# A hybrid-decoder layer on one core: x1 stored earlier, a weight sum made by an adding DMA, products reordered, the last transposes spread out

## The chip, the cores and the metric

The kernel runs on one core of one Trainium2 chip. The metric is the device time of one execution in microseconds, median of the runs. The profile is of one execution.

## The reference, cut to what matters

With DEPTH = 1 only layer 0 runs: sparse attention over a compressed latent, a LayerNorm, a SwiGLU feed-forward, a second LayerNorm. Sequence 256, width 2048, feed-forward width 5632, all float32.

```python
m = _dsa_mixer(x, *mix_p)
x = _layer_norm(DEEPNORM_ALPHA * x + m, ln1_g, ln1_b)          # called x1 below
x = _layer_norm(DEEPNORM_ALPHA * x + (silu(x @ w_gate) * (x @ w_up)) @ w_down, ln2_g, ln2_b)
```

The change touches the feed-forward alone.

## The kernel before, in words

**Splitting.** Every float32 operand is split into a high part (ScalarE, an ACTIVATE Copy to fp32r) and a low part (VectorE, raw minus high), and each product is three matmuls (high x high, high x low, low x high) of 128 x 128 by 128 x 512. A *step* is one weight block of 1024 columns per partition: ScalarE makes its high part, VectorE its low part, TensorE multiplies. The split blocks live in w_hi and w_lo, rings of RING = 4 places. So the high part of step v is made only when TensorE has finished step v - 4, and each engine runs through the steps in one written order, `FFN_STEPS`.

**Gate and up.** The 5632 hidden columns are 22 tiles of 256 (gate and up columns side by side, 512 columns). Tiles 0 and 1 are plain. The other 20 are 10 pairs, p = 1 to 10. In each pair the first four of the 16 inner blocks go by a Strassen-Winograd scheme: seven products in place of eight, over four weight blocks B11, B12, B21, B22 of two 512-column parts, which arrive in one place (`quad`), and sums of them, T1 to T4, made in that place (`pair_sum`, L1378). The remaining 12 blocks are plain steps: six called "first" and six called "second", for the two tiles of the pair. A product step is 6 matmuls, a plain step is 12.

**The sums of weights.** T1 = B11 + B12 replaces B11 and is read by product P5. T3 = B12 + B22 replaces B12 (P7). T2 = T1 + B22 replaces T1 (P6). T4 = T2 + B21 replaces B21 (P4). P1 reads B11, P2 reads B21, P3 reads B22. VectorE makes all four sums and counts them in pair_t_done, and ScalarE's `hi_step` (L955) waits for the count.

**The sums of results.** PSUM is short, so results are passed on by copies. `before_hi` (L972) is what ScalarE does ahead of the high part of step v. The loop there makes three copies per pair ("seeds", semaphore `seeded`), each at the step four places after its product: after P1 it copies the bank second[:, 1] to first[:, 0], after P6 the same bank, negated, to second[:, 0], after P7 the same bank to first[:, 1]. P6 and P7 add into second[:, 1] themselves, so P6 must not begin before the first seed is made, and P7 not before the second. P2 adds into first[:, 0], P3 into second[:, 0], P4 into first[:, 1]. In `pair_product` (L1945) TensorE waits on `seeded` ahead of P6, P7 and P4, and in `pair_plain` (L1968) ahead of "first" 0.

```python
for n, dst, sign in ((P1, first[:, 0, :], 1.0), (P6, second[:, 0, :], -1.0),
                     (P7, first[:, 1, :], 1.0)):
    if v == V_OF[p, "product", n] + RING:
```

The order of a pair p of 2 to 10 is P1, second 3, P5, second 4, P6, second 5, P7, P2, P3, first 0, P4, first 1 to 5, second 0 to 2; the three "second" steps in front belong to pair p - 1. Pair 1 has nothing between: P1, P5, P6, P7, P2, P3, first 0, P4.

**x1 and the factor sums.** The sums of x1 that the products need are made by GpSimd (g_sum) and split by ScalarE (L950) and GpSimd (L1577) into s_gate. s_gate lies on the bytes of xn, which holds x1. So x1 is first stored to DRAM (L669, 2 MB, semaphore x1_stored) and is read back at the end (L682). ScalarE's copy into s_gate stands after the high part of half 6 of tile 1 and waits for the store. SyncE's DMA queue, in order, is: tile 0, the two quad loads of pair 1, tile 1, four plain loads of pair 1 (each waiting for a low part of tile 1), the store of x1, then the rest.

**Down.** The hidden activations of a pair are transposed by VectorE (`turn_hid`, L1341, 16 STREAM_TRANSPOSE in four batches of four), split by ScalarE (`hid_hi`) and VectorE (`hid_lo`), and their sums are made by GpSimd (loop at L1581, with ScalarE's L1003). The down projection runs as 158 units, plain (12 matmuls, 1024 weight columns) or product (3 matmuls, 512 columns); the first four are plain. Of a quad's seven products VectorE makes a weight sum after each of the first four (`t_sum`, L1424). The last pair is transposed in units 3 to 6, a batch in each, its high part is made after unit 8 and its low part before unit 9.

Of the kernel before, what the change touches and what calls it, by code (L numbers as in the profile page):

```python
# [27 lines left out]
ALU = mybir.AluOpType  # L28
# [5 lines left out]
TOK = S // P  # L34
# [117 lines left out]
def ffn_sequence():  # L152

    steps = []
    for p in range(1, PAIRS):
        ends = [(p - 1, "second", n) for n in range(PLAIN - 3, PLAIN)] if p > 1 else [None] * 3
        for product, end in zip((P1, P5, P6), ends):
            steps += [(p, "product", product), end]
        steps += [(p, "product", n) for n in (P7, P2, P3)] + [(p, "first", 0), (p, "product", P4)]
        steps += [(p, "first", n) for n in range(1, PLAIN)] + [(p, "second", n) for n in range(PLAIN - 3)]  # L160
    steps += [(PAIRS - 1, "second", n) for n in range(PLAIN - 3, PLAIN)]
    return tuple(step for step in steps if step)
# [54 lines left out]
DOWN_SLOTS, DOWN_UNITS = down_plan()  # L217
RING_BLOCKS = 2 * RING
LAST_LATE = RING


def ring_places():
# [45 lines left out]
def layer_kernel(nc, a):  # L268
    ctx = ExitStack()
    with ctx:  # L270
# [198 lines left out]
        g_hi = sem("g_hi")  # L469
        g_lo = sem("g_lo")  # L470
        pair_t_done = sem("pair_t_done")
        seeded = sem("seeded")
        y_taken = sem("y_taken")
        y_added = sem("y_added")
# [116 lines left out]
        def _(sp):  # L591
# [71 lines left out]
            for q in range(2):  # L663
                load_quad(1, q)
            load_tile(1)
            for n in range(PLAIN_SLOTS):
                load_plain(1, n)
            sp.wait_ge(x1_done, TOK * CHUNKS)
            sp.dma_start(x1_rows, xn[:]).then_inc(x1_stored, 16)  # L669
            for p in range(1, PAIRS):  # L670
                for n in range(PLAIN_SLOTS if p == 1 else 0, 2 * PLAIN):
                    load_plain(p, n)
# [30 lines left out]
        def _(act):  # L703
# [251 lines left out]
            def hi_step(p, kind, n):  # L955

                v = V_OF[p, kind, n]
                if kind == "product":
                    if n == P1:
                        for q in range(2):  # L960
                            act.wait_ge(quad_full[q], 16 * p)
                    elif n in SUM_OF:
                        act.wait_ge(pair_t_done, 4 * (p - 1) + SUM_OF[n] + 1)
                    act.wait_ge(*used_step(v - RING))
                    act.activation(by_quad(w_hi[:, v % RING, :]), quad(p, SOURCE[n]), ACT.Copy).then_inc(hi_done, 1)  # L965
                else:
                    m = plain_index(p, kind, n)
                    act.wait_ge(plain_full[m % PLAIN_SLOTS], 16 * (m // PLAIN_SLOTS + 1))
                    act.wait_ge(*used_step(v - RING))
                    act.activation(w_hi[:, v % RING, :], plain_raw(m), ACT.Copy).then_inc(hi_done, 1)  # L970
# [50 lines left out]
            for u in range(len(DOWN_UNITS)):  # L1021
                down_hi_unit(u)
                if u == 2:
                    silu_step(TILES - 1)
                if u == 8:
                    hid_hi(PAIRS - 1)
                for pair in range(DOWN_PAIRS):
                    if u == FIRST_REST[2 * pair] + 2:
                        if pair > 0:
                            act.wait_ge(fold_done, FOLDS * pair)  # L1030
                        act.wait_ge(*used_unit(LAST_PRODUCT[pair]))
                        act.activation(hid[:, 0, :, :].rearrange("p t f -> p (t f)"), tp[:, 0, :],
                                       ACT.Copy).then_inc(u2_seeded, 1)
# [11 lines left out]
        def _(dve):  # L1045
# [292 lines left out]
                dve.tensor_tensor(hid[:, i % 2, :, :], hid[:, i % 2, :, :], banks_of(i)[:, :, FC:2 * FC],  # L1338
                                  ALU.mult).then_inc(ffn_hid, 1)

            def turn_hid(p, b):  # L1341

                if b == 0:
                    dve.wait_ge(ffn_hid, 2 * p + 2)
                    dve.wait_ge(y_added, 2 * min(p + 1, PAIRS - 1))
                    if p > 0:
                        dve.wait_ge(s_step, 4 * min(p, len(DOWN_QUADS)))
                for n in range(4):
                    src = hid[32 * n:32 * n + 32, :, :, :].rearrange("p i t (c f) -> p i t c f", c=2)
                    dst = turned[32 * b:32 * b + 32, :, :, :].rearrange("p i c (t s) -> p i t c s", t=TOK)  # L1350
                    last = dve.transpose(dst[:, :, :, :, 32 * n:32 * n + 32], src[:, :, :, :, 32 * b:32 * b + 32])  # L1351
                if b == 3:
                    last.then_inc(ffn_turned, 1)

            def hid_lo(p):
# [45 lines left out]
            for p, kind, n in FFN_STEPS:  # L1401
                before_lo(V_OF[p, kind, n])
                lo_step(p, kind, n)
                if (kind, n) == ("product", P1):
                    pair_sum(p, B11, B11, B12)
                    pair_sum(p, B12, B12, B22)
                if (kind, n) == ("product", P5):
                    pair_sum(p, B11, B11, B22)
                if (kind, n) == ("product", P2):
                    pair_sum(p, B21, B11, B21)  # L1410
                if (kind, n) == ("first", 2):
                    add_y(p)
                if kind == "first" and n >= 2:
                    turn_hid(p - 1, n - 2)
# [49 lines left out]
            for u in range(len(DOWN_UNITS)):  # L1464
                if u == 3:
                    gate_up(TILES - 1)
                if u == 9:
                    hid_lo(PAIRS - 1)
                down_lo_unit(u)
                if DOWN_UNITS[u][4][0] == "product":  # L1470
                    t_sum(u)
                if 3 <= u < 7:
                    turn_hid(PAIRS - 1, u - 3)
                for pair in range(DOWN_PAIRS):
                    rest = u - FIRST_REST[2 * pair]
                    if 3 <= rest < 7:
                        fold(pair, 2 * rest - 6)
                        fold(pair, 2 * rest - 5)
                if u in (FIRST_REST[1] + 3, FIRST_REST[1] + 4):
                    down_residual(0, u - FIRST_REST[1] - 3)  # L1480
                if u in (PAIR_FIRST[1] + 3, PAIR_FIRST[1] + 4):
                    down_residual(1, u - PAIR_FIRST[1] - 3)
# [40 lines left out]
        def _(pool):  # L1523
# [53 lines left out]
            pool.tensor_tensor(s_gate[:, 1, :, :, :], g_sum[:], s_gate[:, 0, :, :, :], ALU.subtract).then_inc(g_lo, 1)  # L1577

            a11, a12, a21, a22 = (turned[:, 0, c, t * P:(t + 1) * P] for t in range(TOK) for c in range(2))
            for q in range(len(DOWN_QUADS)):  # L1580
                if q > 0:  # L1581
                    pool.wait_ge(s_lo, q)
                pool.wait_ge(ffn_turned, q + 1)
                pool.tensor_tensor(s_sum[:, S3, :], a11, a21, ALU.subtract).then_inc(s_step, 1)
                pool.wait_ge(s_step, 4 * q + 1)
                pool.tensor_tensor(a21, a21, a22, ALU.subtract).then_inc(s_step, 1)
                pool.wait_ge(s_step, 4 * q + 2)
                pool.tensor_tensor(s_sum[:, S2, :], a21, a11, ALU.subtract).then_inc(s_step, 1)
                pool.wait_ge(s_step, 4 * q + 3)
                pool.tensor_tensor(s_sum[:, S4, :], a12, s_sum[:, S2, :], ALU.add).then_inc(s_step, 1)  # L1590
                pool.wait_ge(s_hi, q + 1)
                pool.tensor_tensor(s_t[:, q, 1, :, :], s_sum[:], s_t[:, q, 0, :, :], ALU.subtract).then_inc(s_lo, 1)

            pool.wait_ge(xt_full, TOK * CHUNKS)
            pool.affine_select(out=ident[:], in_=ident[:], compare_op=ALU.not_equal, fill=-1.0, base=0,
# [4 lines left out]
        def _(pe):  # L1600
# [344 lines left out]
            def pair_product(p, n):  # L1945

                first, second = banks_of(2 * p), banks_of(2 * p + 1)
                out = {P1: second[:, 1, :], P5: tp[:, 2, :], P6: second[:, 1, :], P7: second[:, 1, :],
                       P2: first[:, 0, :], P3: second[:, 0, :], P4: first[:, 1, :]}[n]
                v = V_OF[p, "product", n]  # L1950
                start = n in (P1, P5)
                if n == P1:
                    pe.wait_ge(ffn_hid, max(1, 2 * p - 2))
                if n == P5:
                    pe.wait_ge(g_lo, 1)
                    if p > 1:
                        pe.wait_ge(y_taken, p - 1)
                if n in (P6, P7, P4):
                    pe.wait_ge(seeded, 3 * p - 2 + (P6, P7, P4).index(n))
                pe.wait_ge(lo_done, v + 1)  # L1960
                for q in range(2):
                    for x, part in ((0, w_hi), (0, w_lo), (1, w_hi)):
                        last = pe.matmul(out, factor(q, Q_FACTOR[n], x), part[:, v % RING, q * GC:(q + 1) * GC],  # L1963
                                         start=(start and (q, x) == (0, 0) and part is w_hi),
                                         stop=((q, x) == (1, 1)), skip_group_check=not start)
                last.then_inc(pe_used, 1)
# [161 lines left out]
```

## Time and profile before

| | us |
|---|---|
| median of 3 runs (lowest, highest) | 940.78 (938.51, 940.89) |
| the profiled execution | 940.2 |
| its span | 938.4 |
| mean granted TensorE clock | 0.998 of full speed |

The span is from the first to the last instruction, and 1.8 us lie around it. Attention and the output projection take the first 224 us, tile 0 and tile 1 run to about 270, the ten pairs to 698 and the down projection to 930. An engine's busy time in a table is not its load: matmuls overlap, and TensorE is busy nearly always in this kernel. What tells of lost time is a gap ahead of a weight load (PEld), and the place where the chain of waits leaves TensorE.

### The profile page before, as it was taken

How to read it: one execution, taken by the hardware profiler on the slowest of the kernel's cores; microseconds unless marked ns; L12 is line 12 of the kernel's file. 1: busy time of each engine (PE TensorE's matmuls, PEld its weight loads, DVE VectorE, ACT ScalarE, POOL GpSimd, SP SyncE). 2: the span in 40 equal slices, each digit the busy share in tenths (PEclk: the TensorE clock that was granted, in tenths of full speed). 3: DMA queues.
4: the chain of work that ended last, by engine and by line, in shares of the span. 5: the costliest groups of instructions: out<-in, count | busy, mean ns of one | idle time of the engine just before them, and what ended most of it. 6: DMA issues, size and time to landing. Idle time of an engine off the chain costs nothing.

```text
span 938.4 us, 11643 instructions
## 1 busy us (share of the span) xinstructions
PE 926.8 (99%) x4406; PEld 775.0 (83%) x4406; DVE 775.2 (83%) x1049; ACT 513.5 (55%) x704; POOL 95.6 (10%) x84
## 2 busy tenths in 40 slices
PE   9999999999989999999999999999999999999997
PEld 8999988888868888888888888888887888888885
DVE  6778566578668898989999999988969987799777
ACT  5686765353445646465565646465545564465550
POOL 0205530000311010202021011000000000000000
PEclk9999999999999999999999999999999999999999
DMA  9844324584617474756647474656665666355632
GB/s 361 317 157 150 121 90 179 180 352 170 213 71 252 129 271 124 258 171 214 231 147 255 125 269 133 248 177 220 224 211 238 257 235 233 133 207 231 236 133 90
DMA packets 36759, 188.06 MB, mean 200 GB/s; under 512 B 4064, under 2 KB 4576, under 8 KB 22880
## 3 DMA queue, kind: packets, MB, share of 16 engines
q1 hardware_dynamic: 36672, 187.32, 55.9%
q8 instruction: 35, 0.57, 0.3%
q14 instruction: 20, 0.16, 0.0%
q0 software_dynamic: 32, 0.00, 0.0%
HBM read 183.11 MB, written 4.19 MB: 200 GB/s over the span
## 4 chain that ended last, share of the span: by engine, by line
PE 94%; DVE 4%; DMA 1%; ACT 1%; issue 0%; DVEq 0%; SPq 0%; ACTq 0%
PE acc L1980 26%; PE acc L2002 19%; PE acc L1755 9%; PE tp L1980 9%; PE acc L1963 6%; PE acc L1693 5%; PE tp L1963 4%; PE acc L1614 4%; PE tp L2002 4%; PE acc L1892 2%; PE acc L1727 1%; DVE w_lo L1204 1%; PE tp L1806 1%; DMA out<-xn 1%; PE tp L1741 1%; DVE turned L1351 1%
## 5 line engine op out<-in xcount | busy, mean ns | idle before, releaser
L1980 PE MATMUL acc<-w_hi,act_t 128*128 128x512 f32 x720 | 227.3, 389 | 0.0
L970 ACT ACTIVATE w_hi<-raw 128x1024 fp32r<-128x1024 f32 x120 | 125.9, 1058 | 108.8 <-PE acc L1980 51.9
L1019 ACT ACTIVATE w_hi<-raw 128x512 fp32r<-128x512 f32 (+1 forms) x154 | 114.7, 782 | 98.4 <-PE acc L2002 83.8
L2002 PE MATMUL acc<-w_hi,hid_t 128*128 128x512 f32 x504 | 161.3, 390 | 0.1
L1422 DVE TENSOR_TENSOR w_lo<-raw,w_hi 128x512 fp32r<-128x512 f32 (+1 forms) x154 | 131.7, 882 | 35.8 <-ACT w_hi L1019 35.4
L1980 PEld LDWEIGHTS acc<-w_hi,act_t 128*128 128x128 f32 x720 | 135.1, 188 | 28.0
L1375 DVE TENSOR_TENSOR w_lo<-raw,w_hi 128x1024 fp32r<-128x1024 f32 x120 | 148.1, 1252 | 6.9 <-ACT w_hi L970 6.1
L1980 PE MATMUL acc<-w_lo,act_t 128*128 128x512 f32 x360 | 140.0, 389 | 0.0
L2002 PEld LDWEIGHTS acc<-w_hi,hid_t 128*128 128x128 f32 x504 | 94.6, 188 | 20.3 <-DVE w_lo L1422 0.8
L2002 PE MATMUL acc<-w_lo,hid_t 128*128 128x512 f32 x252 | 98.1, 389 | 0.0
L1372 DVE TENSOR_TENSOR w_lo<-raw,w_hi 128x1024 fp32r<-128x1024 f32 x63 | 82.8, 1314 | 17.8 <-ACT w_hi L965 17.5
L965 ACT ACTIVATE w_hi<-raw 128x1024 fp32r<-128x1024 f32 x63 | 66.7, 1058 | 46.1 <-DVE raw L1379 31.0
L1351 DVE STREAM_TRANSPOSE turned<-hid 32x256 f32<-32x256 f32 x176 | 76.7, 436 | 3.8
L1980 PEld LDWEIGHTS acc<-w_lo,act_t 128*128 128x128 f32 x360 | 67.6, 188 | 14.1
L1980 PE MATMUL tp<-w_hi,act_t 128*128 128x512 f32 x240 | 76.6, 389 | 0.0
L1755 PE MATMUL acc<-w_hi,o_t 128*128 128x512 f32 x224 | 73.4, 398 | 0.0
L1204 DVE TENSOR_TENSOR w_lo<-raw,w_hi 128x1024 fp32r<-128x1024 f32 x31 | 42.4, 1382 | 22.7 <-ACT w_hi L872 22.7
L2002 PEld LDWEIGHTS acc<-w_lo,hid_t 128*128 128x128 f32 x252 | 47.3, 188 | 9.8
L1980 PEld LDWEIGHTS tp<-w_hi,act_t 128*128 128x128 f32 x240 | 45.0, 188 | 9.3
L1755 PEld LDWEIGHTS acc<-w_hi,o_t 128*128 128x128 f32 x224 | 42.1, 188 | 8.6
L1980 PE MATMUL tp<-w_lo,act_t 128*128 128x512 f32 x120 | 46.7, 389 | 0.0
L1755 PE MATMUL acc<-w_lo,o_t 128*128 128x512 f32 x112 | 43.6, 390 | 0.0
(262 smaller groups left out, 1585.3 us busy)
## 6 DMA issues: line engine op xcount, KB each, us to landing
raw<-in_w_pairs SPq DMA_DIRECT2D x120, 512.0 KB, 4.4
raw<-in_w_down SPq DMA_DIRECT2D x44, 1024.0 KB, 5.7
raw<-in_w_pairs SPq DMA_DIRECT2D x18, 1024.0 KB, 7.6
raw<-in_w_out SPq DMA_DIRECT2D x16, 1024.0 KB, 4.9
raw<-in_w_gu SPq DMA_DIRECT2D x8, 1024.0 KB, 10.3
raw<-in_x_w SPq DMA_DIRECT2D x14, 552.0 KB, 7.1
raw<-in_w_uq SPq DMA_DIRECT2D x4, 1024.0 KB, 6.0
raw<-in_w_ukv SPq DMA_DIRECT2D x4, 1024.0 KB, 4.8
```

Source lines behind the costliest of these rows:

```text
L965: act.activation(by_quad(w_hi[:, v % RING, :]), quad(p, SOURCE[n]), ACT.Copy).then_inc(hi_done, 1)
L970: act.activation(w_hi[:, v % RING, :], plain_raw(m), ACT.Copy).then_inc(hi_done, 1)
L1019: act.activation(unit_parts(u)[0], block_of(b, block, width), ACT.Copy).then_inc(down_hi_done, 1)
L1204: dve.tensor_tensor(w_lo[:, h, 0:n], raw[:, slot, first:first + n], w_hi[:, h, 0:n], ALU.subtract).then_inc(lo_done, 1)
L1351: last = dve.transpose(dst[:, :, :, :, 32 * n:32 * n + 32], src[:, :, :, :, 32 * b:32 * b + 32])
L1372: dve.tensor_tensor(by_quad(w_lo[:, v % RING, :]), quad(p, LOW_OF[n]), by_quad(w_hi[:, v % RING, :]), ALU.subtract).then_inc(lo_done, 1)
L1375: dve.tensor_tensor(w_lo[:, v % RING, :], plain_raw(plain_index(p, kind, n)), w_hi[:, v % RING, :], ALU.subtract).then_inc(lo_done, 1)
L1422: dve.tensor_tensor(lo_, block_of(b, block, width), hi_, ALU.subtract).then_inc(down_lo_done, 1)
L1755: last = pe.matmul(acc[:, bank0 + t, :], lhs[:, k, x, t * P:(t + 1) * P], part[:, w, n * GC:(n + 1) * GC], start=(start and x == 0 and par ...
L1963: last = pe.matmul(out, factor(q, Q_FACTOR[n], x), part[:, v % RING, q * GC:(q + 1) * GC], start=(start and (q, x) == (0, 0) and part is w ...
L1980: last = pe.matmul(out[:, t, :], act_t[:, k0 + m, x, t * P:(t + 1) * P], part[:, v % RING, m * GC:(m + 1) * GC], start=False, stop=(end an ...
L2002: last = pe.matmul(bank, lhs(x), part[:, cols * GC:(cols + 1) * GC], start=(first == u and (cols, x) == (0, 0) and part is hi_), stop=(end ...
```

## The change

- SyncE issues the store of x1 ahead of the four plain loads of pair 1 instead of behind them.
- The order of a pair becomes P1, second 3, P2, second 4, P5, second 5, P6, P7, P3, first 0, P4, and so on; in pair 1 P1, P2, P5, P6, P7, P3, first 0, P4. TensorE waits for the first seed ahead of P2 instead of P6. The three copies of `before_hi` stay as they are, four places after P1, P6 and P7.
- T1 is no longer made by VectorE. GpSimd, once the low part of P1's block is made, issues a DMA that reads B12 from DRAM again (512 KB) and adds it to B11 in place. ScalarE waits for its landing (t1_full) ahead of P5's high part. VectorE makes T4 after P6 instead of after P2.
- GpSimd's loop over the factor sums is cut in two functions, and an adding DMA stands ahead of them in each pair.
- The 16 transposes of the last pair come one in each of units 4 to 19. Its high part is made after unit 22, its low part before unit 23.

```diff
-        for product, end in zip((P1, P5, P6), ends):
+        for product, end in zip((P1, P2, P5), ends):
             steps += [(p, "product", product), end]
-        steps += [(p, "product", n) for n in (P7, P2, P3)] + [(p, "first", 0), (p, "product", P4)]
+        steps += [(p, "product", n) for n in (P6, P7, P3)] + [(p, "first", 0), (p, "product", P4)]
...
+LAST_TURN = 20
...
             load_tile(1)
+            sp.wait_ge(x1_done, TOK * CHUNKS)
+            sp.dma_start(x1_rows, xn[:]).then_inc(x1_stored, 16)
             for n in range(PLAIN_SLOTS):
                 load_plain(1, n)
-            sp.wait_ge(x1_done, TOK * CHUNKS)
-            sp.dma_start(x1_rows, xn[:]).then_inc(x1_stored, 16)
...
+                    elif n == P5:
+                        act.wait_ge(t1_full, 16 * p)
                     elif n in SUM_OF:
-                        act.wait_ge(pair_t_done, 4 * (p - 1) + SUM_OF[n] + 1)
+                        act.wait_ge(pair_t_done, 3 * (p - 1) + SUM_OF[n])
...
-                if u == 8:
+                if u == LAST_TURN + 2:
                     hid_hi(PAIRS - 1)
...
                 if (kind, n) == ("product", P1):
-                    pair_sum(p, B11, B11, B12)
                     pair_sum(p, B12, B12, B22)
                 if (kind, n) == ("product", P5):
                     pair_sum(p, B11, B11, B22)
-                if (kind, n) == ("product", P2):
+                if (kind, n) == ("product", P6):
                     pair_sum(p, B21, B11, B21)
...
-                if u == 9:
+                if u == LAST_TURN + 3:
                     hid_lo(PAIRS - 1)
...
-                if 3 <= u < 7:
-                    turn_hid(PAIRS - 1, u - 3)
+                if LAST_TURN - 16 <= u < LAST_TURN:
+                    b, n = divmod(u - LAST_TURN + 16, 4)
+                    turn_hid(PAIRS - 1, b, (n,))
...
+            def load_t1(p):
+
+                pool.wait_ge(lo_done, V_OF[p, "product", P1] + 1)
+                b12 = by_quad(w_pairs[p - 1][:, 0:2 * RAW_ELEMS])[:, :, B12 * GC:(B12 + 1) * GC]
+                pool.dma_start(quad(p, B11), b12, accum_op=ALU.add).then_inc(t1_full, 16)
...
+            for p in range(1, PAIRS):
+                load_t1(p)
+                if 0 <= p - 2 < len(DOWN_QUADS):
+                    factor_low(p - 2)
+                if p - 1 < len(DOWN_QUADS):
+                    factor_sums(p - 1)
...
-                if n in (P6, P7, P4):
-                    pe.wait_ge(seeded, 3 * p - 2 + (P6, P7, P4).index(n))
+                if n in (P2, P7, P4):
+                    pe.wait_ge(seeded, 3 * p - 2 + (P2, P7, P4).index(n))
```

## Rows read from the trace of the kernel before

**Rows 1.** Busy time and share of the span of each engine, whole execution.
```profile
PE 926.8 (99%) x4406; PEld 775.0 (83%) x4406; DVE 775.2 (83%) x1049; ACT 513.5 (55%) x704; POOL 95.6 (10%) x84
```
**Rows 2.** Waits of weight loads, 262 to 300 us: total, times, longest.
```profile
PEld acc L1963 <- ACT acc L982: 4.2, 2, 2.9
PEld tp L1932 <- DVE w_lo L1204: 1.3, 1, 1.3
```
**Rows 3.** The same view, 696 to 735 us.
```profile
PEld tp L2002 <- DVE w_lo L1422: 1.8, 1, 1.8
PEld acc L2002 <- DVE w_lo L1422: 1.2, 3, 0.5
```
**Rows 4.** Chain of waits, 240 to 292 us: start, duration, what.
```profile
253.00 10.28 DMA out<-xn
...
276.74 2.94 PE acc L1963 x6
...
279.71 0.59 ACT acc L982
...
280.34 4.37 PE acc L1963 x18
...
287.43 1.36 PE acc L1963 x6
```
**Rows 5.** Timeline around tile 1: x1 finished, plain loads, first matmuls of tile 1, s_gate.
```profile
236.80 1.41 DVE L1271 SCALAR_TENSOR_TENSOR xn<-xn,small,ln_rows 128x512 f32<-128x512 f32 x2
...
247.59 5.37 SPq L649 DMA_DIRECT2D raw<-in_w_pairs  x4
...
247.94 0.39 PE L1932 MATMUL tp<-w_hi,act_t 128*128 128x512 f32 x1
...
263.30 1.06 ACT L950 ACTIVATE s_gate<-g_sum 128x1024 fp32r<-128x1024 f32 x1 [5.88 <-DMA out<-xn]
```
**Rows 6.** Chain of waits in pair 3: P1, second 3, second 5.
```profile
394.87 1.36 PE tp L1963 x6
396.23 2.72 PE acc L1980 x12
...
404.39 2.72 PE acc L1980 x12
```
**Rows 7.** Timeline of pair 3: two seeds, silu, a high part; the low part of P1.
```profile
396.33 0.58 ACT L982 ACTIVATE acc<-tp 128x512 f32<-128x512 f32 x1 [0.30 <-PE tp L1963]
...
404.43 0.58 ACT L982 ACTIVATE tp<-tp 128x512 f32<-128x512 f32 x1 [0.30 <-PE tp L1963]
...
407.15 0.60 ACT L933 ACTIVATE hid<-acc 128x512 f32<-128x512 f32 x1 [1.17 <-PE acc L1980]
407.64 1.05 ACT L970 ACTIVATE w_hi<-raw 128x1024 fp32r<-128x1024 f32 x1
...
390.65 1.22 DVE L1372 TENSOR_TENSOR w_lo<-raw,w_hi 128x1024 fp32r<-128x1024 f32 x1
```
**Rows 8.** DMA issues: KB each, median us from issue to landing.
```profile
raw<-in_w_pairs SPq DMA_DIRECT2D x120, 512.0 KB, 4.4
...
rms_g<-in_rms_g_t POOLq DMA_DIRECT2D x1, 3.0 KB, 3.7
```
**Rows 9.** Windows: length, busy of PE, PEld, DVE, ACT, POOL, clock, DMA share, GB/s.
```profile
264.00:282.00 18.00, 13.73 (x51) 9.82 (x51) 15.43 (x13) 9.76 (x12) 2.40 (x1) 0.91 0.00 0
390.00:402.00 12.00, 12.00 (x55) 9.94 (x54) 12.00 (x11) 6.97 (x8) 1.56 (x1) 1.00 0.43 138
```
**Rows 10.** Timeline of VectorE in the first down units.
```profile
702.69 0.69 DVE L1422 TENSOR_TENSOR w_lo<-raw,w_hi 128x512 fp32r<-128x512 f32 x1
703.30 0.69 DVE L1432 TENSOR_TENSOR raw<-raw 128x512 f32<-128x512 f32 x1
704.02 1.78 DVE L1351 STREAM_TRANSPOSE turned<-hid 32x256 f32<-32x256 f32 x4
705.81 0.69 DVE L1422 TENSOR_TENSOR w_lo<-raw,w_hi 128x512 fp32r<-128x512 f32 x1
708.94 1.23 DVE L1422 TENSOR_TENSOR w_lo<-raw,w_hi 128x1024 fp32r<-128x1024 f32 x1
```

More of the change, by code:

```diff
@@ L471, in layer_kernel @@
         pair_t_done = sem("pair_t_done")
+        t1_full = sem("t1_full")
         seeded = sem("seeded")
@@ L1339, in gate_up, with turn_hid @@
                                   ALU.mult).then_inc(ffn_hid, 1)
-            def turn_hid(p, b):
-                if b == 0:
+            def turn_hid(p, b, blocks=range(4)):
+                if b == 0 and 0 in blocks:
                     dve.wait_ge(ffn_hid, 2 * p + 2)
@@ L1347, in turn_hid @@
                         dve.wait_ge(s_step, 4 * min(p, len(DOWN_QUADS)))
-                for n in range(4):
+                for n in blocks:
                     src = hid[32 * n:32 * n + 32, :, :, :].rearrange("p i t (c f) -> p i t c f", c=2)
@@ L1351, in turn_hid @@
                     last = dve.transpose(dst[:, :, :, :, 32 * n:32 * n + 32], src[:, :, :, :, 32 * b:32 * b + 32])
-                if b == 3:
+                if b == 3 and 3 in blocks:
                     last.then_inc(ffn_turned, 1)
@@ L1579, in _, with factor_sums @@
             a11, a12, a21, a22 = (turned[:, 0, c, t * P:(t + 1) * P] for t in range(TOK) for c in range(2))
-            for q in range(len(DOWN_QUADS)):
+            def load_t1(p):
+                pool.wait_ge(lo_done, V_OF[p, "product", P1] + 1)
+                b12 = by_quad(w_pairs[p - 1][:, 0:2 * RAW_ELEMS])[:, :, B12 * GC:(B12 + 1) * GC]
+                pool.dma_start(quad(p, B11), b12, accum_op=ALU.add).then_inc(t1_full, 16)
+            def factor_sums(q):
                 if q > 0:
@@ L1590, in _, with factor_low @@
                 pool.tensor_tensor(s_sum[:, S4, :], a12, s_sum[:, S2, :], ALU.add).then_inc(s_step, 1)
+            def factor_low(q):
                 pool.wait_ge(s_hi, q + 1)
                 pool.tensor_tensor(s_t[:, q, 1, :, :], s_sum[:], s_t[:, q, 0, :, :], ALU.subtract).then_inc(s_lo, 1)
+            for p in range(1, PAIRS):
[4 more added lines that the diff above has]
+                    factor_sums(p - 1)
             pool.wait_ge(xt_full, TOK * CHUNKS)
```

## The prediction

> **What bounds the kernel now.** I read the shares by engine first. TensorE is busy 99% of the span and no other engine over 83% [rows 1], so time is won or lost only where TensorE stops. The view that shows this is the one of waits, read on the weight loads in successive windows: a weight load that stands idle is a real gap. From tile 1 to the end of the down projection there are two places. In pair 1 the weight loads wait 4.2 us on the seed copies of L982 and 1.3 us on a low part of tile 1 [rows 2]. At the start of the down projection they wait 1.8 and 1.2 us on VectorE's low parts [rows 3]. Between 290 and 697 us, nine pairs long, that view has no row: in pair 3 product steps of 1.36 us and plain steps of 2.72 us stand end to end [rows 6], a matmul each 0.227 us. So the change can win in two short places and has nothing to win in nine pairs, where anything that makes TensorE wait costs nine times.
>
> The chain of waits tells the cause in pair 1. The store of x1 takes 10.28 us to land [rows 4]; ScalarE waits 5.88 us for it in front of the s_gate copy [rows 5], and everything behind it is late. Then P6 takes 2.94 us instead of 1.36 at half clock (1.2 GHz, after gaps), and TensorE stands while the second seed is copied [rows 4]. Without any stop P1 would begin 8 x 2.72 us after tile 1's first matmul, at 247.94 + 21.76 = 269.70 [rows 5], and the pair's seven products and first 0 would end 7 x 1.36 + 2.72 = 12.24 us later, at 281.94. They end at 287.43 + 1.36 = 288.79 [rows 4]. Pair 1 loses 6.85 us.
>
> **Store of x1 ahead of the plain loads.** x1 is finished at 236.80 + 1.41 = 238.21, and the first plain load, which the store now precedes on SyncE, is issued at 247.59 [rows 5]. So SyncE's new wait holds up nothing. With the same 10.28 us the store lands near 248.5, and the s_gate copy finds it landed at 263.30 - 5.88 = 257.42 [rows 5]. ScalarE is then early for half 7 of tile 1, the wait of 1.3 us there goes, and P1 runs at 269.70. Were P5 and P6 then as punctual as in later pairs, nearly all of 6.85 us would be won but for the exposed second seed. What is late next is the new DMA.
>
> **The adding DMA, its duration D.** It is issued by GpSimd when P1's low part is made. No accumulating DMA is in this trace. From below: a plain 512 KB load lands in 4.4 us [rows 8]. From above: GpSimd's only DMA takes 3.7 us for 3 KB [rows 8]; this one reads 512 KB from DRAM, reads 512 KB of B11 and writes as much, so at most three times the moving part of a plain load; taking that part as 2.3 us (an estimate, about half of the 4.4) gives 3.7 + 6.9 = 10.6 us. I take 7, between them. In 264 to 282 us the DMA engines are idle, and at 390 to 402 us, where the DMA falls in pair 3, 43% busy [rows 9], so later ones may take a little longer.
>
> **Pair 1 with that DMA.** P1's high part needs half 4 of tile 1, done at 247.94 + 5 x 2.72 = 261.54. High part (1.05) and low part (1.22), durations as in [rows 7], end near 263.9; the DMA lands at L = 263.9 + D. Here stands the wait that is easily missed: the first seed comes four places after P1, in pair 1 that is behind the high parts of P5 and P6, and P2, now second, waits for this seed. The chain is L, high part of P5 1.05, low part 1.2, T2 sum 1.15, high part of P6 1.0, seed 0.6, with handovers of 0.03: P2 starts at L + 5.1. With D = 7 that is 276.0, against 271.06 at which P1 ends: 4.9 us of stop. P2, P5, P6 run to L + 9.2, the second seed is again directly ahead of P7 (0.8 us), and P7, P3, first 0, P4 take 6.8: the end is L + 16.8 = 287.7. A stop of this length was followed by half clock in the trace of before, P6 taking 1.58 us more [rows 4]; I add 1.5. That is 289.2 against 288.79: **+0.4 us**. All that the earlier store wins is spent on the adding DMA. With D = 4.4 it is -2.2, with 10.6 +4.0, and 1.5 less if the clock stays up.
>
> The Trainium skill, "DMA: Bandwidth & Descriptors", section "Anatomy of one DMA — SWDGE (gpsimd) path", puts such a DMA at about 2.0 us plus bytes over 436e3 per us, which is 3.2 us for 512 KB as an estimate; P5 would then not wait for it at all, and pair 1 would come out near -3 us. The DMA that GpSimd issues in this trace speaks against so little, with 3.7 us for 3 KB [rows 8].
>
> **The new order in pairs 2 to 10.** This is the largest term. First seed: made when P1 is done, 396.33 to 396.91 [rows 7], while P2 starts only after second 3, at 396.23 + 2.72 = 398.95. That costs nothing, margin 2 us. Second seed: before, second 5 (2.72 us, [rows 6]) lay between P6 and P7, and the copy of 0.58 us that starts 0.04 us after P6's end (404.43 against 404.39, [rows 6, 7]) was hidden by it. Now P7 follows P6 directly and must wait for this copy. In pair 1 of before the two stand like that, and the chain shows the price: P6 ends at 279.68, the copy runs 279.71 to 280.30, P7 begins at 280.34 [rows 4], 0.66 us. To this comes the lost overlap: a matmul lasts 0.39 us [rows 5] and the next usually begins after 0.23, so 0.16. And ScalarE comes late: at the step of first 0 it has silu and a high part to do after second 5 ends, 407.15 to 408.6 [rows 7], 1.49 us after that end, while P6 now ends 1.36 us after it; with the copy's own 0.04 that is 0.09 more. Together 0.91 us, nine times: **+8.2 us**. From below 9 x 0.66 = 5.9, from above 9 x 1.05 = 9.5. I see no gain in it that could offset this. Third seed: P7 ends 2.3 us after P6's successor could have begun, first 0 needs it two products later, margin some 0.7 us; nothing.
>
> **The adding DMA in pairs 2 to 10.** P1's low part ends at 391.87 [rows 7]. P5 now runs as third product, at 396.23 + 2.72 + 1.36 + 2.72 = 403.03 [rows 6], and needs high and low part, 2.3 us, before: landing by 400.7, so D up to 8.8 us is hidden; the longer chain over T2 to P6 allows 401.4. At 7 it costs nothing; above 8.8 each excess counts nine times. GpSimd's queue behind it: the low factor part and the next factor sums, wanted some 20 us later; nothing. ScalarE behind P5's wait: second 5's high part, a product later; nothing below the same bound. VectorE loses ten sums of 1.15 us, but no step of TensorE waits for it here, so that wins nothing.
>
> **The last transposes.** Before, 16 transposes in four batches of 1.79 us (704.02 to 705.81) fall in units 3 to 6 [rows 10], and units 6 to 12 come late: about 2.9 us [rows 3]. After, they cover units 4 to 19. A transpose costs 0.45 us, and where it follows another instruction 0.11 more: 703.30 to 704.02 is 0.72 where a sum normally takes 0.61 [rows 10]. Single, 16 x 0.56 = 9.0 us instead of 7.6. VectorE's work from 700.9 to the low part of unit 24: 5 plain low parts x 1.14, 16 product low parts x 0.6, 10 sums x 0.6, transposes 9.0, the low part of the hidden values 1.14, in all 31.4, to 732.3, without any wait. TensorE would want unit 24 at 708.87 + 4 x 2.72 + 16 x 0.68 = 730.6. So the debt isn't avoided but moved to units 18 to 24, about 1.7 us and, with VectorE's waits for ScalarE, up to 3. I take **0**, from -2.9 (all gone) to +1.
>
> **The sum.** 940.2 (profiled execution, span 938.4 and 1.8 around it; the median of the runs is 0.6 above it) + 0.4 + 8.2 + 0 = **948.8 us**.
>
> **Rivals.** *The adding DMA is late.* If it takes over 8.8 us beside the plain loads, P5 waits in every pair. At 10.6: pair 1 +4.0, nine times 1.8 = +16.2, seeds +8.2: 968.6. For it: nothing in the trace bounds it well, and GpSimd's DMA is slow for its size. Against: DMA engines are half idle where it falls. Chance 0.22. *The second seed costs little, and the change is faster.* If P7 did not stand for the copy (a seed below 0.1 us of stop per pair), only pair 1 and the down start would count: with D = 5, pair 1 -1.6 and -1.5 for the clock, down -1: 936.1 to 939. It turns faster where the nine stops sum to less than about 4 us. Against it speaks P7 of pair 1, which stands in just this way [rows 4]. Chance 0.08. *The change does less than it says*: the page's short DMA and the down debt all gone give 940.2 + 8.2 - 3.3 - 2.9 = 942.2, the same within what can be told. Chance 0.07. The forecast itself (seed exposed, DMA in time): 0.63.
>
> **How the numbers follow.** About 0.3% (2.8 us) is what a measurement of this kernel can tell from no change. Slower by more: 0.63 + 0.22 = 0.85; within it 0.08; faster 0.07. The forecast's own range runs from 5.9 - 2.2 - 1.5 + 0 to 9.5 + 2.4 (D = 9) + 1, that is 942.4 to 953. Reaching for the late DMA, the range is 943 to 965.
>
> **What would show it.** Ahead of P7 (L1963) nine gaps of near 1 us, released by ScalarE's L982; ahead of P2 in pair 1 a gap of 3 to 8 us with the same releaser, and behind it ScalarE's L965 waiting for GpSimd's DMA; no wait for the store; the DMA's landing time under 9 us; VectorE as the releaser near units 18 to 24. The prediction is wrong if pairs 2 to 10 show no row of waits, or if ScalarE waits for the DMA with weight loads idle behind it in each pair.

## The result and the profile after

| | us |
|---|---|
| before, median of 4 runs | 939.64 (938.3 to 940.89) |
| after, median of 4 runs | 950.61 (950.02 to 950.78) |
| ratio, 95% interval | 1.0116 (1.0100 to 1.0132) |
| span of the profiled execution, before and after | 938.4 and 948.9 |

The change costs 11 us. The times of the kernel before fall in groups by the mean granted clock: in 23 executions of it on one chip those at 1.000 took 937.3 to 938.7 us and those at 0.996 took 940.5 to 941.2, while all four of the changed kernel were at 0.998. Busy shares hardly move; VectorE has ten sums less, GpSimd ten DMAs more:

```profile
PE 928.8 (98%) x4406; PEld 774.4 (82%) x4406; DVE 765.2 (81%) x1039; ACT 515.8 (54%) x704; POOL 108.1 (11%) x94
```

The view that answers to [rows 2, 3] is again the one of the weight loads' waits (who waited for whom, total, times, longest). From 262 to 300, 300 to 708 and 708 to 750 us it says of the changed kernel:

```profile
PEld acc L1985 <- ACT acc L986: 6.1, 2, 5.0
...
PEld tp L1985 <- ACT tp L986: 5.9, 5, 1.2
PEld acc L1985 <- ACT acc L986: 4.7, 4, 1.2
...
PEld acc L2024 <- DVE w_lo L1425: 2.4, 2, 1.2
PEld tp L2024 <- DVE w_lo L1425: 1.1, 1, 1.1
```

L986 is the seed copy (L982 before). The middle pair of rows is new: nine waits of 1.2 us in the stretch that had none. The chain of waits of pair 3 (start, duration, what) answers to [rows 6], and shows one of them. The piece at 405.45 is P5, the one at 406.81 second 5, and the one at 411.66 P7 with P3 behind it:

```profile
405.45 1.36 PE tp L1985 x6
406.81 2.73 PE acc L2002 x12
409.55 0.02 issue
409.57 0.02 ACT hid L935
409.59 0.47 issue
410.06 0.91 ACT w_hi L974
410.97 0.04 issue
411.01 0.60 ACT tp L986
411.61 0.04 issue
411.66 3.02 PE tp L1985 x12
```

The chain leaves TensorE at the end of second 5, goes through silu, the high part of first 0 and the seed on ScalarE and comes back at P7. P6 itself runs beside it and isn't in the chain. In the timeline P6's last matmul starts at 410.50 and P7's first at 411.66: 1.16 us where 0.23 is usual.

Pair 1, the same view:

```profile
263.99 6.22 DMA quad<-in_w_pairs
270.21 0.02 issue
270.23 1.07 ACT w_hi L969
271.30 0.02 issue
271.32 1.23 DVE w_lo L1376
272.55 1.15 DVE quad L1383
...
274.68 0.59 ACT acc L986
275.27 0.04 issue
275.31 2.82 PE acc L1985 x6
278.13 1.78 PE tp L1985 x6
...
287.68 1.36 PE acc L1985 x6
```

The store of x1 has left the chain of [rows 4], and the adding DMA stands in its place: it lands 6.22 us after its issue, then come P5's high part, its low part, the T2 sum, P6's high part, and at last the first seed, for which P2 waits 5.0 us. P2 takes 2.82 us instead of 1.36 after that stop, and P5 1.78: the granted clock was 0.58 from 275 to 278 us and 0.78 from 278 to 280. P4 ends at 289.04, against 288.79 before.

The sums agree: pair 1 +0.25; nine pairs at a distance of (671.05 - 325.16) / 8 = 43.24 us between the P7s of pairs 2 and 10, against 42.16, +9.7; start of the down projection 3.5 us of waits instead of 3.0, +0.5. That is 10.45 of the 10.5 us of span.

The DMA issues (KB each, median us to landing) answer to [rows 8]:

```profile
raw<-in_w_pairs SPq DMA_DIRECT2D x120, 512.0 KB, 4.7
raw<-in_w_pairs POOLq DMA_DIRECT2D x9, 512.0 KB, 6.1
out<-xn SPq DMA_DIRECT2D x1, 2048.0 KB, 10.0
```

### The profile page after: what moved, and what is told of

It is laid out like the page before. It is cut to its first block, busy times and chain, and to the rows that moved or that the text cites. A ratio compares the mean times of both kernels' runs of the same rounds, so it can differ in the third digit from the quotient of the medians.

```text
span 948.9 us, 11643 instructions
## 1 busy us (share of the span) xinstructions
PE 928.8 (98%) x4406; PEld 774.4 (82%) x4406; DVE 765.2 (81%) x1039; ACT 515.8 (54%) x704; POOL 108.1 (11%) x94
## 4 chain that ended last, share of the span: by engine, by line
PE 93%; DVE 3%; ACT 2%; issue 1%; DMA 1%; DVEq 0%; ACTq 0%
PE acc L2002 26%; PE acc L2024 18%; PE acc L1777 9%; PE tp L2002 9%; PE acc L1985 5%; PE acc L1715 5%; PE acc L1636 4%; PE tp L1985 4%; PE tp L2024 3%; PE acc L1914 2%; DVE w_lo L1425 2%; PE tp L1954 1%; PE acc L1749 1%; PE tp L1828 1%; ACT w_hi L974 1%
## 5 line engine op out<-in xcount | busy, mean ns | idle before, releaser
L1379 DVE TENSOR_TENSOR w_lo<-raw,w_hi 128x1024 fp32r<-128x1024 f32 x120 | 148.1, 1253 | 22.5 <-ACT w_hi L974 21.4
L1376 DVE TENSOR_TENSOR w_lo<-raw,w_hi 128x1024 fp32r<-128x1024 f32 x63 | 76.3, 1222 | 22.2 <-ACT w_hi L969 22.1
L1208 DVE TENSOR_TENSOR w_lo<-raw,w_hi 128x1024 fp32r<-128x1024 f32 x31 | 41.7, 1361 | 17.5 <-ACT w_hi L874 17.5
```

The costliest lines, as they stand in the source:

```text
L1376: dve.tensor_tensor(by_quad(w_lo[:, v % RING, :]), quad(p, LOW_OF[n]), by_quad(w_hi[:, v % RING, :]), ALU.subtract).then_inc(lo_done, 1)
L1379: dve.tensor_tensor(w_lo[:, v % RING, :], plain_raw(plain_index(p, kind, n)), w_hi[:, v % RING, :], ALU.subtract).then_inc(lo_done, 1)
```

## The experiments

Each kernel is compared with the kernel before, run on the same chip; ratios are with their 95% interval.

**Which part costs what.** First the changed kernel with one part undone: VectorE makes T1 again.

```diff
-                    elif n == P5:
-                        act.wait_ge(t1_full, 16 * p)
...
-                        act.wait_ge(pair_t_done, 3 * (p - 1) + SUM_OF[n])
+                        act.wait_ge(pair_t_done, 4 * (p - 1) + SUM_OF[n] + 1)
...
+                    pair_sum(p, B11, B11, B12)
...
-                load_t1(p)
```

> The changed kernel with one part undone: VectorE makes T1 again, no adding DMA; order, store and turning as changed. Theory (the second seed stands exposed between P6 and P7): the nine gaps ahead of P7 in pairs 2 to 10 stay, 1.18 us each on the weight loads, pair pitch 43.2 us. Pair 1: the stop ahead of P2 shrinks from 5.0 to about 1.1 us, because ScalarE's high part of P5 can start at 266.7 and not at 270.2; end of P4 near 284 instead of 289. Total about 945.2. Rival (the adding DMA makes the nine gaps, by holding up ScalarE or by its traffic): the gaps vanish, pitch 42.2, total about 935.

Measured 945.66 us, 1.0070 (1.0051 to 1.0090). The nine waits stand there unchanged, without any adding DMA:

```profile
PEld tp L1964 <- ACT tp L982: 5.9, 5, 1.2
PEld acc L1964 <- ACT acc L982: 4.7, 4, 1.2
```

So the theory holds and its rival falls. The DMA's own price is 950.61 - 945.66 = 5.0 us, all in pair 1, where the stop ahead of P2 is 1.5 instead of 5.0 us and the half clock stays away (P2 takes 1.66 us and P4 ends at 284.05, 4.99 earlier).

The store alone, on the kernel before:

```diff
+            sp.wait_ge(x1_done, TOK * CHUNKS)
+            sp.dma_start(x1_rows, xn[:]).then_inc(x1_stored, 16)
             for n in range(PLAIN_SLOTS):
                 load_plain(1, n)
-            sp.wait_ge(x1_done, TOK * CHUNKS)
-            sp.dma_start(x1_rows, xn[:]).then_inc(x1_stored, 16)
```

> The kernel before with the one edit on the store of x1 (issued ahead of the plain loads of pair 1). Theory: P1 runs near 269.5, stops of about 0.8 us ahead of P6 and 1.2 us ahead of P7 are left, P4 of pair 1 ends near 284 instead of 288.8, nothing else changes: total about 4.8 us under the kernel before, 935. Rival (the store was not what held pair 1, the chain through VectorE's sums was): gain under 2 us.

Measured 934.20 us, 0.9948 (0.9929 to 0.9967), 4.6 under the kernel before. P4 of pair 1 ends at 282.97. Of the two stops expected only the one ahead of P7 is left, 1.1 us. The two traces are 5.8 us apart at that point; in the one of the kernel before, P6 ran at half clock, which it doesn't do in every execution (last section). This part of the change is a gain, hidden in the whole by the rest.

The order alone, on the kernel before:

```diff
-        for product, end in zip((P1, P5, P6), ends):
+        for product, end in zip((P1, P2, P5), ends):
...
-        steps += [(p, "product", n) for n in (P7, P2, P3)] + [(p, "first", 0), (p, "product", P4)]
+        steps += [(p, "product", n) for n in (P6, P7, P3)] + [(p, "first", 0), (p, "product", P4)]
...
-                if (kind, n) == ("product", P2):
+                if (kind, n) == ("product", P6):
...
-                if n in (P6, P7, P4):
-                    pe.wait_ge(seeded, 3 * p - 2 + (P6, P7, P4).index(n))
+                if n in (P2, P7, P4):
+                    pe.wait_ge(seeded, 3 * p - 2 + (P2, P7, P4).index(n))
```

> The kernel before with the new order of the products alone: VectorE's T1, store and turning as before. Theory: nine gaps of 1.18 us ahead of P7, pitch 43.2, 9.5 us; in pair 1 the first seed now stands ahead of P2, behind the high parts of P5 and P6, about 1 us more than before. Total near 949.6. Rival (nine gaps need the early store or the other turning as well): total under 945.

Measured 951.47 us, 1.0132 (1.0115 to 1.0148). The nine waits are there again (5.9 in five, 4.7 in four). In pair 1 the first seed costs 4.4 us ahead of P2, and P4 ends at 290.32, 1.5 later than before, a little more than expected. The order by itself costs as much as the whole change (1.0132 against 1.0116, and the intervals overlap).

The turning alone, on the kernel before:

```diff
-                if 3 <= u < 7:
-                    turn_hid(PAIRS - 1, u - 3)
+                if 4 <= u < 20:
+                    b, n = divmod(u - 4, 4)
+                    turn_hid(PAIRS - 1, b, (n,))
```

> The kernel before with the 16 last transposes one by one in units 4 to 19, high part after unit 22, low part before unit 23, nothing else. Theory (VectorE's debt is moved, and single transposes cost 0.1 us more each): gaps of 3.4 us near units 19 to 24 in place of 2.9 us near 9 to 12, total 0.5 us above the kernel before, so the same as can be told. Rival (spreading frees TensorE): gaps under 1 us, total about 2 us under before.

Measured 938.84 us, 1.0001 (0.9989 to 1.0013). The waits are those forecast, three of 1.15 us. They are 0.4 us more than before, too little for the times to show:

```profile
PEld acc L2003 <- DVE w_lo L1422: 2.3, 2, 1.2
PEld tp L2003 <- DVE w_lo L1422: 1.1, 1, 1.1
```

The adding DMA alone, in the old order:

```diff
+                    elif n == P5:
+                        act.wait_ge(t1_full, 16 * p)
...
-                        act.wait_ge(pair_t_done, 4 * (p - 1) + SUM_OF[n] + 1)
+                        act.wait_ge(pair_t_done, 3 * (p - 1) + SUM_OF[n])
...
-                    pair_sum(p, B11, B11, B12)
...
+                pool.wait_ge(lo_done, V_OF[p, "product", P1] + 1)
+                b12 = by_quad(w_pairs[p - 1][:, 0:2 * RAW_ELEMS])[:, :, B12 * GC:(B12 + 1) * GC]
+                pool.dma_start(quad(p, B11), b12, accum_op=ALU.add).then_inc(t1_full, 16)
```

> The kernel before with T1 made by the adding DMA, in the old order (P5 directly after one plain step), store and turning as before. Theory: with 6.1 us to landing, P5 is late in each of pairs 2 to 10. It wants T1 by 396.6 in pair 3, the DMA lands near 398.5: 1.5 to 2 us of gap ahead of P5, none ahead of P7, and in pair 1 some 4 us. Total near 958, above the changed kernel. Rival (the DMA is hidden in this order too and only the new order costs): total within 941 to 944.

Measured 980.37 us (974.2 to 983.0), 1.0417 (1.0384 to 1.0449): the direction was right and the size by 22 us too small. From 300 to 740 us the weight loads wait twice per pair:

```profile
PEld tp L1983 <- issue: 17.8, 9, 2.5
PEld acc L2000 <- DVE w_lo L1378: 7.5, 5, 1.8
PEld tp L2000 <- DVE w_lo L1378: 6.2, 4, 1.8
```

The first row is P5, 2.0 us each on average, as expected (the view names no releaser, the low part of P5 comes last). The other two were not in the expectation: the plain step after P5 waits 1.5 us more, since on VectorE its low part stands behind P5's low part and the T2 sum. The two make 31.5 us over nine pairs, pair 1 another 4.1. Most of the rest goes with the clock: it was 0.74 from 264 to 290 us in pair 1, three of the later pairs ran partly at half clock after these stops, and of the four executions the one with the highest mean clock (0.995) was the shortest and the one with the lowest (0.983) the longest.

```profile
412.00:460.00 48.00, 45.22 (x187) 36.37 (x186) 37.64 (x43) 23.62 (x28) 7.43 (x6) 0.93 0.60 187
460.00:506.00 46.00, 42.91 (x188) 34.92 (x187) 37.64 (x43) 23.88 (x28) 7.48 (x6) 1.00 0.61 195
```

The column after the five engines is the granted clock. The first stretch, at 0.93, holds a pair of 48.0 us (P5 starts at 414.25 and, in the next pair, at 462.29), the second one of 45.8. So in the old order the adding DMA stops TensorE in every pair. The new order hides it, and has a price of its own, 9.7 us in pairs 2 to 10. The DMA gives nothing back for it there: with VectorE's T1 the pairs stand 43.22 us apart, with the DMA 43.24.

**What the nine waits are.** If P7 waits only for the seed copy, 2.72 us of other work between P6 and P7 must remove the wait. In the changed kernel:

```diff
-        for product, end in zip((P1, P2, P5), ends):
+        for product, end in zip((P1, P2), ends):
             steps += [(p, "product", product), end]
-        steps += [(p, "product", n) for n in (P6, P7, P3)] + [(p, "first", 0), (p, "product", P4)]
+        steps += [(p, "product", P5), (p, "product", P6), ends[2]]
+        steps += [(p, "product", n) for n in (P7, P3)] + [(p, "first", 0), (p, "product", P4)]
```

> The changed kernel with one step moved: the third of the plain steps between the products stands between P6 and P7 instead of between P5 and P6. Adding DMA as changed. Theory: the 2.72 us of that step hide the seed, the nine gaps vanish, pitch 42.16, if T1 lands in time: P6's low part needs landing plus 5.7 us, the margin is about 0.5 us with a landing after 6.2 us. Pair 1 unchanged. Total 950.6 - 9.5 = 941. Rival (DMA makes the gaps): gaps of about 1 us stay, now ahead of P5 or P6, total near 950.

Measured 952.06 us, 1.0143 (1.0123 to 1.0162), where 941 was expected. The waits ahead of P7 are gone, and yet nothing is won: in their place TensorE waits for low parts, ahead of P6 and of the plain step after it.

```profile
PEld acc L2003 <- DVE w_lo L1380: 4.2, 4, 1.1
PEld tp L2003 <- DVE w_lo L1380: 3.8, 4, 1.0
PEld tp L1986 <- DVE w_lo L1377: 3.2, 4, 1.1
PEld acc L1986 <- DVE w_lo L1377: 2.4, 3, 0.8
```

These stops stand in pairs 2 to 8. Pair 9 has one of 0.7 us and pair 10 none, with the same adding DMA and the same order. What sets pairs 2 to 8 apart is VectorE's T2 sum, 2.04 us long in pair 3 and 1.22 in pair 9 (its reason comes below). So the late landing of T1 and the slow sum bind together. The run didn't settle what the nine waits are. The same move on the run with VectorE's T1, so with the same diff and no adding DMA, does:

> The run with VectorE's T1 and the changed order, store and turning, and the third plain step between the products moved between P6 and P7. Only this step's place differs from the run with VectorE's T1 (945.66 us, nine gaps of 1.18). Theory (P7 stood for the seed copy, nothing else): T2 is in time without the DMA, 2.72 us hide the copy, all nine gaps vanish and no other comes, pair pitch 42.16, total 945.7 - 9.5 = 936.1. Rival (the gap only moves, ahead of P6 or of a plain step, for want of ScalarE's or VectorE's time): a gap of 0.5 to 1 us stays in each pair, total 941 to 945.

Measured 938.05 us, 0.9990 (0.9980 to 1.0000), 7.6 under the run with VectorE's T1, where 9.5 less was expected. All nine waits of 1.2 us are gone: the seed copy between P6 and P7 was their cause. Seven of 0.4 us are left, in pairs 2 to 8, ahead of the plain step:

```profile
PEld acc L1982 <- DVE w_lo L1376: 1.7, 4, 0.4
PEld tp L1982 <- DVE w_lo L1376: 1.3, 3, 0.4
```

Pairs 2 to 8 are those in which GpSimd makes the low part of the factor sums. The timeline of pair 3 has it beside VectorE's T2 sum, which takes 2.04 us where the same sum takes 1.22 in pairs 9 and 10:

```profile
395.38 2.04 DVE L1380 TENSOR_TENSOR raw<-raw 128x1024 f32<-128x1024 f32 x1
...
394.69 1.64 POOL L1594 TENSOR_TENSOR s_t<-s_sum,s_t 128x384 fp32r<-128x384 f32 x1 [9.31 <-ACT s_t L1004]
```

To try this, ScalarE's copy of the sums was moved from behind P5 to behind P4:

```diff
-                if (kind, n) == ("product", P5) and 2 <= p < len(DOWN_QUADS) + 2:
+                if (kind, n) == ("product", P4) and 2 <= p < len(DOWN_QUADS) + 2:
```

> The last covered run (VectorE's T1, a plain step between P6 and P7, 938.05 us, gaps of 0.43 in pairs 2 to 8 and none in 9 and 10), with ScalarE's copy of the factor sums after P4 instead of after P5, so that GpSimd's low part of them no longer falls beside VectorE's T2 sum. Theory (the sum reads SBUF beside GpSimd and takes 2.04 us instead of 1.22, which makes plain step second 5 late): the sum falls to 1.22 in all pairs, the seven gaps vanish, total near 935.5. Rival (VectorE's order, with the T4 sum ahead of the plain step, is late by itself): the seven gaps stay.

Measured 936.74 us, 0.9970 (0.9960 to 0.9980), where 935.5 was expected. The sum falls to 1.22 us and no row of VectorE is left from 290 to 700 us. A small new wait comes, 0.24 us ahead of first 0 in the same seven pairs, since ScalarE's copy now stands ahead of the third seed:

```profile
394.36 1.22 DVE L1380 TENSOR_TENSOR raw<-raw 128x1024 f32<-128x1024 f32 x1
...
PEld acc L1982 <- ACT acc L983: 1.7, 7, 0.2
```

The Trainium skill, "SBUF — State Buffer", section "Who interferes with whom", states that a VectorE instruction with two SBUF inputs contends with a GpSimd instruction that reads SBUF. The two rows of 2.04 and 1.22 us agree.

**What of the wait is ScalarE's backlog.** In the changed kernel the second seed one step earlier, ahead of silu and the high part of first 0:

```diff
-                        if v == V_OF[p, "product", n] + RING:
+                        if v == V_OF[p, "product", n] + RING - (n == P6):
```

> The changed kernel with ScalarE's second seed one step earlier in its order, ahead of silu and of the high part of first 0. Theory: the gap ahead of P7 is the copy (0.58), handovers and lost overlap, and 0.1 us of it is ScalarE still at work; so each gap falls from 1.18 to about 1.08 us and the total by about 1 us to 949.7. Rival (ScalarE's backlog is most of the gap): gaps fall below 0.7 us, total under 946.

Measured 956.23 us, 1.0186 (1.0166 to 1.0205), 5.6 above the changed kernel, where 1 us less was expected. Ahead of P7 the wait falls from 1.18 to 1.09 us, as the theory said and the rival didn't. But a second wait opens behind it:

```profile
PEld acc L2002 <- ACT acc L986: 7.0, 9, 0.8
PEld tp L1985 <- ACT tp L986: 5.5, 5, 1.1
PEld acc L1985 <- ACT acc L986: 4.4, 4, 1.1
```

The first row is first 0, waiting for the third seed. Silu, first 0's high part, the y copy and P4's high part now all stand between the second and the third seed on ScalarE, and the 0.7 us of margin that the prediction gave to the third seed are used up.

**A version that beats both.** The early store alone leaves three places. The transposes were spread wider, one in every third unit from 4 to 49:

```diff
-                if 3 <= u < 7:
-                    turn_hid(PAIRS - 1, u - 3)
+                if 4 <= u < 52 and (u - 4) % 3 == 0:
+                    b, n = divmod((u - 4) // 3, 4)
+                    turn_hid(PAIRS - 1, b, (n,))
```

> The kernel before with the store of x1 early, and the 16 last transposes one in every third unit from 4 to 49, high part after unit 51, low part before unit 52. Theory: per quad VectorE needs 8.9 us where TensorE takes 10.2, so 1.3 us are free per quad and three transposes of 0.56 are 1.7; the small debt is taken from its early lead and no gap of over 0.3 us is left in the down stage. Gain 2.9 us on the run with the early store alone (934.2), 931.3 us. Rival (VectorE has no time to spare in the quads at all): gaps of 2 to 4 us near units 30 to 52.

Measured 932.04 us, 0.9922 (0.9908 to 0.9937). The waits of the down projection fall from 3.0 to 1.0 us (0.6 the longest, at 760 us), not to under 0.3 each as expected. Then, on top of it, every fourth unit, and in pair 1 alone P2 between P6 and P7:

```diff
-        steps += [(p, "product", n) for n in (P7, P2, P3)] + [(p, "first", 0), (p, "product", P4)]
+        steps += [(p, "product", n) for n in ((P2, P7, P3) if p == 1 else (P7, P2, P3))] + [(p, "first", 0), (p, "product", P4)]
```

> The run with early store and spread turning (932.04 us), with two more edits: in pair 1 alone P2 stands between P6 and P7, and the 16 transposes come one in every fourth unit (4 to 64), high part after unit 65, low part before 66. Theory: P2's 1.36 us hide the second seed, the gap of 1.09 us in pair 1 goes; three gaps of together 1.0 us in the down stage go: total near 930.1. Rival (the third seed or the low part of P2 is late in turn, or the hidden values come too late for tile 20): no gain, 932 or more.

Measured 930.56 us, 0.9906 (0.9892 to 0.9920). From 200 to 900 us one row is left:

```profile
PEld acc L1964 <- issue: 0.4, 1, 0.4
```

## Why the prediction was right, point by point

*Pair 1.* Forecast +0.4, measured +0.25. The store was hidden as reckoned (landing 10.0 us, the s_gate copy at 256.86), and the adding DMA took its place. D was put at 7 us from the end of P1's low part; it was 6.5 in pair 1 (263.69 to 270.21), of which issue to landing were 6.2. In pair 3 the low part ends at 393.91 and ScalarE starts on T1 at 400.46, 6.55 us. From the landing on, the chain was exact: P2 starts 5.1 us later, at 275.31, and stood 5.0 us where 4.9 was reckoned. Small errors then cancel: T1 landed at 270.21 and not at 270.9, and P2 and P5 took 1.9 us more at lowered clock where 1.5 was put. There is some luck in it as well. The +0.4 counts half clock on both sides, and the kernel before has it in some executions only: in the run with the turning alone, whose pair 1 is the same, a like stop ahead of P6 left the clock at 1.00 and P6 took 1.66 us.

*The short DMA.* By the Trainium skill's "DMA: Bandwidth & Descriptors", section "Anatomy of one DMA — SWDGE (gpsimd) path", it would be 3.2 us, as an estimate. The trace doesn't agree: 6.1 us from issue to landing, about twice as long. No run here has a plain DMA of this size from GpSimd, so how much of the difference is the addition stays open.

*Pairs 2 to 10.* The largest term: forecast 8.2, measured 9.7, just above the 9.5 that the prediction gave as its upper bound. The mechanism was right, the term too small: 1.08 us per pair (43.24 against 42.16) instead of 0.91. The stop itself was reckoned well. From the end of P6's last matmul (410.50 + 0.39 = 410.89) to P7's start at 411.66 are 0.77 us, where 0.66 and 0.09 of backlog were put; with the early seed it is 0.67, so the backlog is confirmed. The lost overlap of 0.16 holds too. What the sum left out is the start after a stop. P7's first matmul is followed after 0.33 us (411.66, 411.99) and not 0.23, and P7 and P3 fill 3.02 us of the chain where 12 matmuls usually fill 2.72, so 0.30 instead of 0.16. A row in [rows 4] had shown it: 4.37 us for 18 matmuls of 0.227, which is 0.28 more.

*The adding DMA in pairs 2 to 10.* Hidden, as forecast: 6.55 us against a bound of 8.8. Where one plain step of this margin is taken away (the run with the cover), T1 is late together with the slow T2 sum. The third seed's margin of 0.7 us was real as well: the early seed used it up. The prediction has first 0 two products behind P7, but only P3 lies between; the third seed ends at 413.93 and first 0 begins at 414.51, so 0.6 us are left.

*The last transposes.* Forecast 0 with a debt moved to units 18 to 24; measured +0.5, three waits at the forecast place (ahead of units 18, 19 and 24, by the order of the units). The run with this part alone can't be told from no change.

*The rivals.* The late DMA, the cheap seed and the change that does less than it says did not come. The forecast of 948.8 us for the sum was 1.8 under the median, 1.5 of it the seed term. The wider range of the prediction ends at 965, below the 968.6 of its own late rival; nothing hung on it.

## What to carry to other kernels

When steps are reordered, write down for each copy between them who waits for it now and how much other work lies between: a copy of 0.6 us between two adjacent steps costs a full 1.1 us each time, and one that stands in an engine's order behind a late transfer can cost most of the transfer (5.0 us of 6.2 here). A wait removed at one place opened another in three of the runs (the two covers and the early seed), so a reorder is worth checking at all its waits. And where several edits come together, time each alone: here a gain of 4.6 us was buried under a loss of 16 (950.6 against 934.2 for the store alone).

## What the runs showed of the hardware that was not expected

An accumulating DMA of 512 KB, issued by GpSimd, took 6.1 us to land (median of nine) beside 4.7 for a plain load of the same size from SyncE. Of it 1.2 us were GpSimd's own instruction.

Stops of 1.0 to 2.5 us, two per pair, left the clock at full speed in five of the eight stretches measured in the run with the DMA alone and lowered it in three (0.93 over 48 us, each pair one to two us longer). The stops don't tell which: behind stops of 2.5 and 1.8 us the clock was 1.00 from 368 to 374 us, behind those of 2.3 and 1.6 in the next pair it was 0.60 from 414 to 420 us. The same holds for the kernel before. Its pair 1 has a stop of 2.9 us ahead of P6, and so has the run with the turning alone, which differs only behind the pairs; the windows behind it, before and turning alone:

```profile
276.00:282.00 6.00, 4.59 (x13) 3.22 (x14) 5.90 (x7) 4.15 (x6) 0.00 (x0) 0.72 0.00 0
276.00:282.00 6.00, 5.26 (x22) 4.04 (x23) 5.48 (x5) 5.24 (x8) 0.00 (x0) 1.00 0.00 0
```

The column after the five engines is the granted clock, 0.72 and 1.00; P6 took 2.94 us in the one and 1.66 in the other. So equal stops did not always cost the same, and two single executions can differ by 1.3 us at this place alone.
